# Grid attention's merge gate: from plain float32 products inside its scans to three float32r products in an earlier stage

## The reference

```
u = h @ w_in                                  # columns: a_q a_k a_v | b_z b_xbc b_dt | c_q c_k c_v | gates (3 x 1024)
ya = window_attention(...)                    # 8 heads of 64
ys = rms_norm((yf + yb + xs * d) * silu(b_z)) # state space branch, width 1024
yg = grid_attention(rope(rms(c_q)), rope(rms(c_k)), c_v, ...)   # dense softmax over 1280 keys
ga, gb, gc = split(sigmoid(gates))
m = ga * (ya @ w_oa) + gb * (ys @ w_ob) + gc * (yg @ w_oc)
x = x + gate1 * (m @ w_out)
```

## Time and profile before

| | us |
|---|---|
| median of 3 runs | 4710.16 (4707.54 to 4710.68) |
| the profiled execution, its own time | 4710.8 |
| its span, first to last instruction | 4709.0 |
| TensorE busy | 4294.7 |
| VectorE busy | 2364.7 |
| ScalarE busy | 1534.7 |

### The profile page before, as it was taken

One profiled execution on the slowest core, in us unless ns is written; L12 is line 12 of the kernel. 1 busy time (PEld: TensorE's weight loads), 2 busy tenths in 40 slices (PEclk: granted clock), 3 DMA queues, 4 the chain that ended last, 5 costly groups with the idle time before them and its releaser, 6 DMA issues.

```text
span 4709.0 us, 46130 instructions
## 1 busy us (share of the span) xinstructions
PE 4294.7 (91%) x18454; PEld 3089.6 (66%) x18454; DVE 2364.7 (50%) x3770; ACT 1534.7 (33%) x2958; POOL 901.2 (19%) x695
## 2 busy tenths in 40 slices
PE   7896889998999999988889998899888998999997
PEld 3455754756788888645457856555665657888886
DVE  2778864253556653335362337554666734333334
ACT  3465641123211111332333125342544623222222
POOL 2112224121344441015151000011000021000001
PEclk9997899999999999888989999999999999999998
DMA  5112243012334331221211201011000031111111
GB/s 192 44 57 85 83 127 112 27 45 81 99 105 118 112 112 50 104 60 40 63 45 46 80 33 36 27 63 41 23 23 18 19 116 36 54 45 51 42 42 63
DMA packets 257800, 308.90 MB, mean 66 GB/s; under 512 B 19072, under 2 KB 209936, under 8 KB 256304
## 3 DMA queue, kind: packets, MB, share of 16 engines
q1 hardware_dynamic: 238096, 227.15, 15.7%
q0 software_dynamic: 17408, 75.64, 5.1%
q10 hardware_dynamic: 2080, 3.15, 0.2%
HBM read 271.61 MB, written 34.28 MB: 65 GB/s over the span
## 4 chain that ended last, share of the span: by engine, by line
PE 61%; DVE 10%; ACT 5%; issue 1%; POOL 1%; DMA 1%; POOLq 0%; DVEq 0%; ACTq 0%
PE bank L193 60%; PE bank L196 2%; DVE Mx L205 1%; ACT Mx L202 1%; ACT at21P L202 1%; ACT at20P L202 1%; POOL sq L205 1%; DVE at21sm L223 1%; DVE at20sm L223 1%; DVE x L211 0%; DMA wslot<-in_w_in 0%; DVE wfl L205 0%; DVE at11sm L223 0%; DVE at21Pl L205 0%; DVE at10sm L223 0%
## 5 line engine op out<-in xcount | busy, mean ns | idle before, releaser
L193 PE MATMUL bank<-h,wslot 128*128 128x512 f32 (+2 forms) x1616 | 689.9, 565 | 32.8 <-DMA wslot<-in_w_in 19.1
L193 PE MATMUL bank<-hT,wslot 128*128 128x512 f32 (+3 forms) x1136 | 462.3, 564 | 16.7 <-DVE hT L211 7.3
L193 PEld LDWEIGHTS bank<-h,wslot 128*128 128x128 f32 (+1 forms) x1616 | 290.6, 190 | 262.3 <-issue 245.7
L193 PEld LDWEIGHTS bank<-hT,wslot 128*128 128x128 f32 (+1 forms) x1136 | 212.3, 190 | 242.4 <-issue 237.3
L193 PE MATMUL bank<-ffn1h,wfh 128*128 128x512 f32 x704 | 279.8, 398 | 11.8 <-DVE ffn1l L211 10.9
L211 DVE SCALAR_TENSOR_TENSOR x<-bank,mod,x 128x512 f32<-128x512 f32 x224 | 164.4, 746 | 245.1 <-PE bank L193 244.8
L193 PE MATMUL bank<-ffn2h,wgh 128*128 128x512 f32 x704 | 276.4, 393 | 9.6 <-DVE ffn2l L211 9.2
L193 PE MATMUL bank<-ffn1l,wfh 128*128 128x512 f32 x704 | 275.1, 391 | 0.0
L193 PE MATMUL bank<-ffn2l,wgh 128*128 128x512 f32 x704 | 274.9, 390 | 0.0
L193 PE MATMUL bank<-ffn2h,wgl 128*128 128x512 f32 x704 | 274.9, 390 | 0.0
L193 PE MATMUL bank<-ffn1h,wfl 128*128 128x512 f32 x704 | 274.5, 390 | 0.0
(11 more groups left out here) (555 smaller groups left out, 9412.9 us busy)
## 6 DMA issues: line engine op xcount, KB each, us to landing
wslot<-in_w_in SPq DMA_DIRECT2D x40, 1024.0 KB, 5.7
ffn1t<-in_w_mod POOLq DMA_DIRECT2D x64, 512.0 KB, 4.8
wslot<-in_w_ffn_in SPq DMA_DIRECT2D x44, 512.0 KB, 5.4
Mx<-acsT SPq DMA_DIRECT2D x32, 512.0 KB, 4.9
at1w<-in_ada_w POOLq DMA_DIRECT2D x24, 512.0 KB, 4.7
wslot<-in_ffn_w_gate SPq DMA_DIRECT2D x22, 512.0 KB, 4.1
wslot<-in_ffn_w_up SPq DMA_DIRECT2D x22, 512.0 KB, 5.3
wslot<-in_w_ffn_out SPq DMA_DIRECT2D x20, 512.0 KB, 5.4
```

The lines of the kernel that those rows point to most:

```text
L193: return Counted() if counting[0] else self.q.matmul(o, l, r, start=start, stop=stop)
```

## The change

The gate of grid attention leaves att2. The list ZT gets eight more column blocks, c, between z and g. They are made as z and g are, by three float32r products; ScalarE takes their sigmoid into the ring zr, and GpSimd writes it to a new tensor gspill2. GpSimd's sums of squares are now laid between these writes, and the norm's steps, which stood at g 2 and g 3, stand at c 2 and c 3. In att2 the early gate tiles, the gate matmuls, their copies, writes and weight loads are gone, and the output ring bo has two banks in place of one (bg's bank is free there). In mg2 ScalarE has nothing to do, since the gate comes in with its sigmoid taken; VectorE waits for the load. Window attention and mg1 stay as they are.

```diff
-    gins = [Sem(f"gin{i}", 16) for i in range(8)]
-    ZT = [(kind, m) for kind in "zgo" for m in range(8)]
+    gins, gc_outs = [Sem(f"gin{i}", 16) for i in range(8)], [Sem(f"gco{i}", 16) for i in range(3)]
+    ZT = [(kind, m) for kind in "zcgo" for m in range(8)]
...
     def sz_sp(e, tiles):
-                w, c = (w2, 768) if kind == "z" else (w2, 4128 + 1024) if kind == "g" else (io["w_ob_2"], 0)
+                w, c = (w2, 768) if kind == "z" else (w2, 4128 + 1024) if kind == "g" else (w2, 4128 + 2048) if kind == "c" else (io["w_ob_2"], 0)
...
     def sz_pe(e):
-            st = sz if kind == "z" else mg0
+            st = sz if kind in "zc" else mg0
...
-            if kind == "g" and m in (0, 2):
+            if kind == "c" and m in (0, 2):
                 rms_y.sum_pe(e, *LAT[m // 2])
 
     def sz_pool(e):
-        rms_y.pool(e)
+
+        for m in range(8):
+            if m < 2:
+                rms_y.sums(e, *LAT[m])
+            for n0, n in LAT:
+                e.wait_ge(*sz.act.after("c", m, n0))
+                o = gc_outs[zr.place.get(("c", m, n0), 0) % 3]
+                e.dma_start(io["gspill2"][:, m * NL + n0:m * NL + n0 + n], zr["c", m, n0][:, 0:n]).then_inc(o("c", m, n0), 16)
+                zr.give(("c", m, n0), o.now())
...
     def sz_act(e):
-                if kind == "z":
-                    zz = zr.take(m, n0)
+                if kind in "zc":
+                    zz = zr.take(kind, m, n0)
...
-                    e.activation(zz[:, 0:n], bk_z["z", m, n0][:, 0:n], AF.Silu).then_inc(sz.act("z", m, n0), 1)
+                    e.activation(zz[:, 0:n], bk_z[kind, m, n0][:, 0:n], AF.Silu if kind == "z" else AF.Sigmoid).then_inc(sz.act(kind, m, n0), 1)
...
     class Merge:
-            for x in self.att.g_out:
-                e.wait_ge(*x.now())
+            for x in (self.att.g_out if self.br == 1 else gc_outs):
+                e.wait_ge(*x.end())
...
-                    e.dma_start(gb[:, 0:n], io["gspill"][:, m * NL + n0:m * NL + n0 + n]).then_inc(self.gate_in(m, n0)(self.br, m, n0), 16)
+                    e.dma_start(gb[:, 0:n], io["gspill" if self.br == 1 else "gspill2"][:, m * NL + n0:m * NL + n0 + n]).then_inc(self.gate_in(m, n0)(self.br, m, n0), 16)
...
     def act(self, e):
-            for m, n0, n in self.blocks:
+            for m, n0, n in self.blocks if self.br == 1 else ():
...
     def dve(self, e):
-                e.wait_ge(*st.act.after("g", m, n0))
+                e.wait_ge(*(st.act.after("g", m, n0) if self.br == 1 else self.gate_in(m, n0).after(self.br, m, n0)))
...
     class AttGroup:
-            self.bs, self.bt, self.bo, self.bg = Ring(bank[0:4]), Ring(bank[4:6]), Ring(bank[6:7]), Ring(bank[7:8])
+            self.bs, self.bt, self.bo, self.bg = Ring(bank[0:4]), Ring(bank[4:6]), Ring(bank[6:7 if self.win else 8]), Ring(bank[7:8])
...
-            self.places = [(1, 2, 3, 4), (0, 1, 2, 3)] if self.win else [(2, 4, 5, 6), (0, 2, 4, 6)]
-
-            self.early = 1 if self.win else 2
+            self.places = [(1, 2, 3, 4), (0, 1, 2, 3)]
+            self.early = 1 if self.win else 0
...
     def gate_pe(self, e, i, j):
-            if b > 7 or j not in self.places[i % 2]:
+            if not self.win or b > 7 or j not in self.places[i % 2]:
...
     def sp(self, e, ahead):
             load(e, (self.nm, "q"), [(w2, 0, 8, self.at.q0 + g * 256, 256, 0)])
+            if not self.win:
+                ahead(e)
+                return
...
     def proj_pe(self, e):
-                if not self.win and j >= len(self.items):
-                    self.gate_early_pe(e, j - len(self.items))
```

More of the change, by code:

```diff
@@ L488, in pool, with sums @@
             for n0, n in self.rngs:
[L489 to L494, removed]
+                self.sums(e, n0, n)
+        def sums(self, e, n0, n):
+            for k in range(1, self.first + 1):
+                sq, was = sqr[self.nm, n0, k][:, 0:n], sqr[self.nm, n0, k - 1][:, 0:n]
+                e.wait_ge(*self.st.act.after(self.nm, "sq", n0, k))
+                e.wait_ge(*(self.st.pool.after(self.nm, "sq", n0, k - 1) if k > 1 else self.st.act.after(self.nm, "sq", n0, 0)))
+                e.tensor_tensor(sq, sq, was, OP.add).then_inc(self.st.pool(self.nm, "sq", n0, k), 1)
+                sqr.give((self.nm, n0, k - 1), self.st.pool.now())
         def mean_dve(self, e, n0, n):
@@ L3290, in sz_act @@
         cut_act(e, 2)
-        for t, (kind, m) in enumerate(ZT[0:16]):
+        for t, (kind, m) in enumerate(ZT[0:24]):
             if (kind, m) == ("g", 7):
@@ L3298, in sz_act @@
             for n0, n in LAT:
-                if kind == "z":
-                    zz = zr.take(m, n0)
-                    for ev in zr.freed(m, n0):
+                if kind in "zc":
+                    zz = zr.take(kind, m, n0)
+                    for ev in zr.freed(kind, m, n0):
                         e.wait_ge(*ev)
-                    e.wait_ge(*sz.pe.after("z", m, n0))
-                    e.activation(zz[:, 0:n], bk_z["z", m, n0][:, 0:n], AF.Silu).then_inc(sz.act("z", m, n0), 1)
-                    bk_z.give(("z", m, n0), sz.act.now())
+                    e.wait_ge(*sz.pe.after(kind, m, n0))
+                    e.activation(zz[:, 0:n], bk_z[kind, m, n0][:, 0:n], AF.Silu if kind == "z" else AF.Sigmoid).then_inc(sz.act(kind, m, n0), 1)
+                    bk_z.give((kind, m, n0), sz.act.now())
                 else:
@@ L3314, in sz_act @@
                 rms_y.square(e, *LAT[t - 7])
-            if (kind, m) == ("g", 2):
+            if (kind, m) == ("c", 2):
                 rms_y.roots(e)
-        for t in range(18, 24):
+        for t in range(26, 32):
             cut_act(e, t)
@@ L3340, in sz_dve @@
                     e.wait_ge(*sz.act.after("z", m, n0))
-                    e.tensor_tensor(a, a, zr[m, n0][:, 0:n], OP.mult).then_inc(sz.dve("z", m, n0), 1)
-                    zr.give((m, n0), sz.dve.now())
+                    e.tensor_tensor(a, a, zr["z", m, n0][:, 0:n], OP.mult).then_inc(sz.dve("z", m, n0), 1)
+                    zr.give(("z", m, n0), sz.dve.now())
             if t:
                 cut_dve(e, t + 2)
-            if (kind, m) == ("g", 2):
+            if (kind, m) == ("c", 2):
                 for n0, n in LAT:
                     rms_y.mean_dve(e, n0, n)
-            if (kind, m) == ("g", 3):
+            if (kind, m) == ("c", 3):
                 for n0, n in LAT:
@@ L3361, in sz_dve @@
             if m < 6:
-                cut_dve(e, 18 + m)
+                cut_dve(e, 26 + m)
     drop(m1)
@@ L3515, in gate_act @@
             c = self.early + i // 2
-            if c > 7 or i % 2 == 0 or j != self.places[1][3] + 1:
+            if not self.win or c > 7 or i % 2 == 0 or j != self.places[1][3] + 1:
                 return
@@ L3868, in __init__ @@
             self.q0, self.k0, self.v0 = (0, 512, 640) if self.win else (3360, 3872, 4000)
-            self.gcol = 4128 + (1, 0, 2)[br] * 1024
-            self.g_out = att1.g_out if br == 2 else [Sem(f"gout{i}", 16) for i in range(3)]
+            if self.win:
+                self.gcol, self.g_out = 4128, [Sem(f"gout{i}", 16) for i in range(3)]
             self.st, self.bk = Stage(f"av{br}"), Ring(bank)
@@ L4216 @@
     io["gspill"] = nc.dram_tensor("gspill", (128, 8 * NL), _mybir.dt.float32, kind="Internal").ap()
+    io["gspill2"] = nc.dram_tensor("gspill2", (128, 8 * NL), _mybir.dt.float32, kind="Internal").ap()
     io["hspill"] = nc.dram_tensor("hspill", (128, 8 * TT), _mybir.dt.float32, kind="Internal").ap()
```

## The result

The changed kernel takes 4784.4 us (median of 4 runs, 4781.0 to 4790.4) against 4710.4 for the kernel before (4 runs, 4707.5 to 4717.7). The ratio is 1.0153, 95% interval 1.0136 to 1.0170: slower, and 3 us above the forecast of 4781. The profiled execution is the slowest of the four, 4790.4 us, so a few microseconds of what its trace shows beyond the change are not the change's.

What follows compares the result with a forecast made beforehand. TensorE was taken to bound the gate stage without slack, and a ring of waits between three engines the gate-free units of grid scans. 4710.8 + 88.8 - 25.2 + 7 + 1 = 4782.4, forecast 4781 us, range 4769 to 4797.

Steps and rivals of the forecast that it cites:

- The added tiles: Gate stage: 16 new tiles at 5.547 us each are paid in full, +88.8 us; their writes cost 0.
- The rival of writes that hold up the tiles: Gate stage: a sigmoid waits for its buffer and TensorE stops, up to 8 us, giving 4789; chance 0.05.
- The removal: Grid attention's scans without gate work: 337.2 us for both instead of 362.4, -25.2 us, stall included.
- The yardstick: Grid scans: distance between rsx copies is a unit's time; a unit without gate work takes 11.34 us.
- The clock: Thinner grid scans: 12 of 28 intervals lose 0.58 us to a lower granted clock, +7 us, bounds 0 and 16.
- The rival of scans that cool down for good: Grid scans: each of 28 intervals pays one or two low-clock stretches, 16 or 32 us, giving 4791 to 4807; chance 0.13.
- The edges: Scan edges: cold swap products cost +3.4 us, first units gain 2.4; together +1 us, bounds -6 and +6.
- The second bank: Grid attention's output ring: nothing waits for the bank, so a second one is worth 0.
- The rival that decided the sign the other way: Grid scans: a second output bank breaks the ring of waits, units fall to 8.70 us, giving 4700; chance 0.03.
- The merge: Grid attention's merge: loses 16 sigmoids but stays at TensorE's 128 matmul records, 55.19 us; change 0.
- The sum: Whole kernel, profiled execution: 4710.8 + 88.8 - 25.2 + 7 + 1 = 4782.4 us; median of runs 4781, 1.5% slower.

Runs made afterwards that it cites:

- fillers: Changed kernel with one output bank plus two matmuls per unit, read by nobody, in grid attention's scans: 4775.1 us, ratio 1.0145.
- The earlier load: Kernel before, each attention group's second gate weight load issued before the third gate tile's write instead of the fifth's: 4690.0 us, ratio 0.9956.
- better places: Kernel before with that weight load moved and odd units' gate matmuls in grid scans at steps 2, 4, 5, 6: 4684.7 us, ratio 0.9931.

## Why the prediction was right, point by point

**The added tiles.** Counted 88.8 us, measured 88.9 in the chain and 88.2 between two kernels that differ in them and in an output bank that is worth nothing. The stage was TensorE's without a hole and is so still. The writes through GpSimd cost nothing: they land in 2.3 us, and TensorE's waits in the stage are those it had. The Trainium skill's estimate for such a write (DMA: Bandwidth & Descriptors, "Anatomy of one DMA — SWDGE (gpsimd) path"), 2.6 us, was near the 2.3 us of this trace. The rival of writes that hold up the tiles is dead.

**The removal.** The yardstick, units without gate work in the kernel before, was right to 0.01 us: 11.34 then, 11.33 now. Counted -25.2 for the steady part and +7 for the clock, -18.2; measured -19.1. With the clock held up it is 362.4 - 333.2 = 29.2, more than the 25.2, because the last unit of a scan also saw the slow clock in the yardstick (9.84 us at a granted clock of 0.65 there, 7.92 at 1.00 with fillers). The earlier load shows what part of this was not the price of the gate's matmuls: 9.4 us was a late weight load, which one moved line removes. The gate's 96 matmuls in the scans, some 83 us of TensorE's time (eight of them lie ahead of the first copies), cost 353.0 - 343.3 = 9.7 us of the path, and 3.1 with better places. Against scans whose clock is held up (333.2) it is 19.8 and 13.2.

**The clock.** Counted as 12 of 28 units at 0.58 us, +7. Measured: 14 of the 28 were longer than 11.33, by 0.3 to 0.6 us, 7.0 us in all; the two last units were 3.2 us longer than with fillers. That a thinner scan would lose clock in some units was read from the trace. That it would be 12 was a guess from two units, one of which had paid, and that the count came out at 7.0 us has luck in it: more units paid less each. The fillers show it as a cause and not only as a reading: the waits are for the same engines but shorter, the clock is 1.00, and no unit is long. It cost 14 of the 28 units something, not each: nearly equal waits at 3426 and 3437 us left the clock up once and took it down once, and what decides between the two was not found. The Trainium skill (TensorE: Matmul & The Clock Gate, "HAM oscillation — how this bites in real kernels") describes a loop in which every turn starts cold, because in each turn a wait for data stands that is longer than the turn's matmuls. The units here are another case, as their trace shows: the waits, 1.4 and 0.8 us, are short beside the 11.3 us of a unit, and half of the units kept the clock. The rival of scans that cool down for good is refuted by the granted clock of 0.90 and 0.93.

**The edges.** Counted +3.4 for four cold swap products and -2.4 for the first units. TensorE idled 7.38 and 8.24 us before the two swap products of each group, as foretold (7). The first score of a group came 1.90 us later after the group's start in both groups, 3.8 for the four, which is 0.95 each (2.08 against 1.12 us). The first units gained 1.5 and 0.5 us. Together +1.8 where +1 was counted.

**The second bank**, counted at nothing, is nothing. The rival that decided the sign the other way had only this to stand on.

**The merge** took 55.19 us in both.

**The sum** was 4782.4 for the profiled execution, which came out at 4790.4; the difference is mainly in three stages that the change leaves alone (+2.8, +4.0, +2.9 us), of which 5.8 us are the two dense stretches that began at 1.2 GHz, and the median of the runs lies at 4784.4. The sum knew nothing of such stretches; that they stayed small is luck. What the first 2.8 us are is open. Two figures behind the sum are rounded a little wrong: 4782.4 less 0.6 is 4781.8, not 4781, and the low end of the range comes to 4768 by the prediction's own terms (4710.8 + 88.8 - 25.2 - 6), not 4769. Neither changes a reading.

## What to carry to other kernels

Before moving work from one stage to another, read the slack of both: 88.8 us of dense matmuls in a stage that TensorE fills cost 88.8, while 110 us in a stage that goes by waits between engines gave back 17.3 us when they went (28.6 with the fillers, which keep the clock up). Units of the same loop that happen to lack the work are the best estimate of what removing it gives, stalls around it counted apart: here 9.4 of the 25.2 us that were counted as gain was a weight load issued too late. And where TensorE is thinned out, count what it loses in clock; work that fills its gaps can be better than free.

## What the runs showed of the hardware

- The same 128 matmul records, with TensorE busy all through, took 55.19 us in one trace and 58.12 in another: the second began at 1.2 GHz (0.51 over its first 6 us) and the first at 2.4 GHz (1.00), behind the same wait of 1.75 us for VectorE.
- Two useless matmuls per unit, 1.5 us of TensorE's time, made a loop of 11.3 us units faster by some 0.3 us per unit: the granted clock of the scans went from about 0.91 to 1.00.
- A plain float32 matmul of 128x512 costs 0.86 us at 2.4 GHz (6.9 us for eight), three float32r ones 0.69 us (5.547 us for 24). As work the new form was a fifth cheaper; the placement undid it. Form and place were changed together: three float32r products at the old places, inside the scans, were not tried.
- The same kernel's runs spread by 0.2 to 0.5% (4702 to 4725 us for the kernel before on one chip), so effects of a few microseconds had to be read in stages of the trace.
